# Seven-product projections: how the summed weight quarters are made, and by which engine

## The chip, the cores and the metric

One core of one Trainium2 chip runs the kernel. The metric is the device time of one execution in microseconds (us). TensorE multiplies, VectorE, ScalarE and GpSimd work elementwise, SyncE issues plain loads, and the 16 DMA engines move data; accumulating transfers (destination += source) are issued by GpSimd.

## The reference

Two decoder-like blocks on 512 tokens of width 1024, all in fp32: a first block (gated linear attention, dilated attention, MLP, an embedding gate) and a second block (mLSTM with stick-breaking attention, then a pooling layer). The part that matters is in `even_layer`: the projections that make the gates o and z of the mLSTM, two products of the normalised activations h (512 x 1024) with columns of one weight:

```
u = h @ w_in_ab                      # (512, 1024) @ (1024, ...)
o, z = 1024 columns each of u        # gates of the mLSTM's output
a = head_rmsnorm(sigmoid(o) * mlstm(q, k, v, ...)) * silu(z)
```

## The kernel before

Every fp32 matmul is made of three passes in a reduced format: each operand is split into a high part and a low part (the rest), and TensorE adds hi x hi, hi x lo, lo x hi. Weights come as blocks of 128 x 512 (256 KB). A block is loaded (SyncE, L605) into one of `RING` = 8 slots of `w_raw`, cast to `w_hi` by ScalarE (L766), and GpSimd subtracts that from the raw block to make `w_lo`, in two halves of 256 columns (`rest`, L713). `w_hi` and `w_lo` have 8 slots too; a cast of block b waits until TensorE has used block b - 8 (`wait_used`), a load until the low part of the block 8 places earlier in the ring is made (`wait_lo`). Each engine runs its queue in the order in which it is written; `prepare` and `prepared_to` say how far ScalarE's casts have to be at a place of its queue.

The gates o and z are made in another way. For each of the two, a class `Seven` splits the 1024 x 1024 weight into quarters q11, q12, q21, q22 (each 4 blocks) and the activations likewise, and replaces eight quarter products by seven, in the order B11, T1, T2, B21, T3, B22, T4. Their right operands are q11, q11+q12, q11+q12+q22, q21, q12+q22, q22, q11+q12+q22+q21. A product is 4 blocks x 2 token tiles x 3 passes = 24 matmuls (L2472 to L2474). Two products before it in TensorE's order have used its eight slots.

How the right operands are made before:

- `kept` (4 blocks in the arena) is loaded with q11 (L615) and is B11. When B11's low part of block k is made, GpSimd issues an accumulating DMA of q12 into it (`weight_sums`, L744), which gives T1; when T1's low part is made, another of q22, which gives T2. Each is waited for by the cast (`kept_summed`).
- B22 (q22) and T3's q12 come through the ring; VectorE adds the second to the first (`add_t3`, L2048).
- B21 is loaded into `b21`; VectorE adds it to `kept` for T4 (`add_t4`, L2053).
- All 28 low parts of a slab are made by VectorE (`rests`, L2063), the sums between them.

The partial results pass between products: ScalarE copies B11's result into the banks of T2 (`b_from_a`, L1280), VectorE adds T2's result and T1's copy into the banks of B22 (`c_from_b`, L2074), and T3's result to the copy (`own_from_b`, L2081). ScalarE's gate functions (L1307) and VectorE's products (L2096, L2101) take the four quarters of the result. In z's slab ScalarE also computes the squares of the heads (L1342) and a root, with two table loads. In front of the two slabs stands sb_q (8 blocks of 12 matmuls), behind them sb_k, whose low parts GpSimd makes again, and in which TensorE transposes the gated result (L2498).

Of the kernel before, what the change touches and what calls it, by code (L numbers as in the profile page):

```python
# [233 lines left out]
def plan_raw(blocks):  # L234
# [4 lines left out]
    for s, j in blocks:  # L239
        kind = "seven" if isinstance(s, Seven) else "plain"  # L240
        made[kind] += 1
        lo_at.append((kind, made[kind]))
        p, k = j // 4, j % 4
        if kind == "seven" and p not in (T3, B22):
            place.append(("b21" if p == B21 else "kept", k))
            loads.append({B11: ("kept", k, 16 * (group + 1)), T1: ("kept_sum", k, 16 * (2 * group + 1)),
                          T2: ("kept_sum", k, 16 * (2 * group + 2)), B21: ("b21", k, 16 * (group + 1)),
                          T4: ("added", 0, 8 * group + 4 + k + 1)}[p])
        else:
# [4 lines left out]
            if kind == "seven" and p == T3:  # L254
                t3_loads[len(loads)] = slots[slot]
                loads.append(("added", 0, 8 * group + k + 1))
            else:
                loads.append(("ring", slot, slots[slot]))
# [4 lines left out]
def two_blocks(nc, W, out):  # L263
# [12 lines left out]
    with ctx:  # L276
# [124 lines left out]
        for s in sevens:  # L401
            s.kept, s.b21, s.own = view(0, 4, NCOL), view(10240, 4, NCOL), view(2048, 2, NCOL)
# [28 lines left out]
        kept_summed, b21_loaded = [sem(f"kept_summed{k}") for k in range(4)], [sem(f"b21_loaded{k}") for k in range(4)]  # L431
# [112 lines left out]
        def raw_of(b):  # L544

            where, at = place[b]
            return w_raw[:, at, :] if where == "ring" else (blocks[b][0].b21 if where == "b21" else blocks[b][0].kept)[:, at, :]

        def wait_raw(eng, b):
# [3 lines left out]
                        {"ring": raw_loaded, "kept": kept_loaded, "kept_sum": kept_summed, "b21": b21_loaded}[what][at], n)  # L553
# [46 lines left out]
        def _(sp):  # L600
            def load(b, src):
                if ring_no[b] >= RING:
                    wait_lo(sp, ring_order[ring_no[b] - RING])
# [4 lines left out]
            def load_seven(s):  # L608
                at = sevens.index(s)
                if s is sevens[0]:  # L610
# [78 lines left out]
        def _(pool):  # L689
# [63 lines left out]
        def _(act):  # L753
# [557 lines left out]

            o_, z_ = sevens
# [23 lines left out]
            width = D // 4  # L1336

            def head_squares(r0):
                for r in range(r0, r0 + 8):
                    sq_ = squares[:, r // 2, (r % 2) * width:(r % 2 + 1) * width]  # L1340
                    h_ = lstm_h[:, r // LSTM_HEADS, (r % LSTM_HEADS) * LSTM_HD:(r % LSTM_HEADS + 1) * LSTM_HD]
                    ins = act.activation(sq_, h_, ACT.Square, accum_out=stat[:, r:r + 1])  # L1342
                return ins

            head_squares(0)
            prepared_to(z_, T3, 3)
            step(head_squares(8))
            act.activation(root[:], stat[:], ACT.Sqrt, bias=eps_col[:, 0:1], scale=1.0 / width).then_inc(head_root_ready, 1)
# [156 lines left out]
        def _(vec):  # L1505
# [538 lines left out]
            def add_t3(s, k):  # L2044
                own, other = s.first_of(T3) + k, s.first_of(B22) + k
                vec.wait_ge(raw_loaded[place[own][1]], t3_loads[own])
                wait_raw(vec, other)
                vec.tensor_tensor(raw_of(own), raw_of(own), raw_of(other), ALU.add).then_inc(block_added, 1)  # L2048

            def add_t4(s, k):  # L2050
                wait_raw(vec, s.first_of(B21) + k)
                wait_lo(vec, s.first_of(T2) + k)
                vec.tensor_tensor(s.kept[:, k, :], s.kept[:, k, :], s.b21[:, k, :], ALU.add).then_inc(block_added, 1)  # L2053

            def rests(s, p, k):
                while seven_made[0] < s.first_of(p) + k:
                    b = seven_made[0]
                    if lo_at[b][0] == "seven":
                        own, j = blocks[b]
                        if j // 4 == B21:  # L2060
# [930 lines left out]
```

## Time and profile before

| | |
|---|---|
| median of 3 runs | 1937.35 us (1936.15 to 1937.51) |
| profiled execution, its time | 1936.78 us |
| its span | 1935.0 us |
| busy: TensorE, weight loads | 99%, 83% |
| busy: VectorE, ScalarE, GpSimd | 41%, 42%, 49% |
| mean DMA rate over the span | 96 GB/s |

The profile is of one execution. Times in it count from the start of the span; busy shares are of the whole span, and the two slabs that the change touches run from about 1239 to 1324 us of it.

### The profile page before, as it was taken

The numbers are of one execution on the slowest core, as the hardware profiler recorded it, in microseconds if no ns is written. First come the engines' busy times: TensorE is split into PE (matmuls) and PEld (weight loads), VectorE is DVE, ScalarE is ACT, GpSimd is POOL, SyncE is SP. The second block draws the span as 40 slices with busy tenths as digits, with TensorE's granted clock in tenths as the row PEclk, the third lists the DMA queues.
The fourth block names the chain that finished last, engine by engine and source line by source line (L and its number), as shares of the span: only waits on it lengthen the run. The fifth ranks groups of instructions, "written<-read, shape, count | busy, mean of one in ns | idle before, by whom it ended". The sixth has DMA issues, their size and how long they took to land.

```text
span 1935.0 us, 25859 instructions
## 1 busy us (share of the span) xinstructions
PE 1915.9 (99%) x9142; PEld 1607.0 (83%) x9142; DVE 790.0 (41%) x1264; ACT 811.0 (42%) x1585; POOL 951.1 (49%) x1237
## 2 busy tenths in 40 slices
PE   9999999999999999999999999999999999999998
PEld 7878888998888988888889888877888888888887
DVE  2430321340123223323247854766356646014652
ACT  5522443423324333333356543355456646333332
POOL 5733544534365555665545733115344455555572
PEclk9999999999999999999999999999999999999999
DMA  6342433323133323333342320554222242333331
GB/s 233 104 107 54 123 88 87 88 66 85 57 109 109 121 88 92 100 106 103 98 131 70 106 76 23 131 136 125 61 77 71 71 136 74 101 92 93 96 111 54
DMA packets 102849, 186.44 MB, mean 96 GB/s; under 512 B 11068, under 2 KB 16808, under 8 KB 102750
## 3 DMA queue, kind: packets, MB, share of 16 engines
q1 hardware_dynamic: 94676, 170.41, 30.1%
q10 hardware_dynamic: 5770, 10.49, 1.7%
q0 software_dynamic: 2304, 4.20, 1.3%
q8 instruction: 64, 1.05, 0.2%
q14 instruction: 35, 0.29, 0.0%
HBM read 179.03 MB, written 6.02 MB: 96 GB/s over the span
## 4 chain that ended last, share of the span: by engine, by line
PE 90%; DVE 5%; ACT 2%; DMA 2%; issue 1%; POOL 0%; SPq 0%; DVEq 0%; ACTq 0%; POOLq 0%
PE proj L2325 26%; PE proj L2327 26%; PE proj L2326 26%; DMA arena<-in_w_in_ab 2%; PE work L2325 1%; PE work L2326 1%; PE work L2327 1%; PE work L2896 1%; PE work L2877 1%; DVE w_lo L2063 1%; PE work L2701 1%; ACT w_hi L766 1%; PE work L2498 1%; PE work L2852 1%; PE work L2420 1%
## 5 line engine op out<-in xcount | busy, mean ns | idle before, releaser
L713 POOL TENSOR_TENSOR w_lo<-w_raw,w_hi 128x256 fp32r<-128x256 f32 x1200 | 931.9, 809 | 877.6 <-ACT w_hi L766 761.8
L2325 PE MATMUL proj<-act_hi,w_hi 128*128 128x512 f32 (+1 forms) x1312 | 495.8, 378 | 0.6 <-DVE arena L1775 0.3
L2327 PE MATMUL proj<-act_hi,w_lo 128*128 128x512 f32 (+1 forms) x1312 | 490.4, 374 | 0.0
L2326 PE MATMUL proj<-act_lo,w_hi 128*128 128x512 f32 (+1 forms) x1312 | 490.3, 374 | 0.0
L766 ACT CAST w_hi<-w_raw 128x512 fp32r<-128x512 f32 x520 | 304.1, 619 | 398.9 <-PE proj L2327 369.7
L2325 PEld LDWEIGHTS proj<-act_hi,w_hi 128*128 128x128 f32 x1312 | 247.1, 188 | 44.6 <-DVE arena L1775 0.7
L2327 PEld LDWEIGHTS proj<-act_hi,w_lo 128*128 128x128 f32 x1312 | 247.0, 188 | 44.3
L2326 PEld LDWEIGHTS proj<-act_lo,w_hi 128*128 128x128 f32 x1312 | 247.2, 188 | 43.7 <-issue 0.5
L2325 PE MATMUL proj<-w_hi,act_hi 128*128 128x512 f32 x640 | 257.5, 402 | 1.2 <-DVE arena L2187 1.0
L2327 PE MATMUL proj<-w_hi,act_lo 128*128 128x512 f32 x640 | 250.2, 391 | 0.0
L2326 PE MATMUL proj<-w_lo,act_hi 128*128 128x512 f32 x640 | 249.9, 391 | 0.0
L2325 PEld LDWEIGHTS proj<-w_hi,act_hi 128*128 128x128 f32 x640 | 128.0, 200 | 25.3 <-issue 2.1
L2325 PE MATMUL proj<-w_hi,aux_hi 128*128 128x512 f32 x368 | 146.1, 397 | 2.9 <-ACT arena L904 1.9
L2327 PEld LDWEIGHTS proj<-w_hi,act_lo 128*128 128x128 f32 x640 | 128.0, 200 | 23.1
L2326 PEld LDWEIGHTS proj<-w_lo,act_hi 128*128 128x128 f32 x640 | 128.2, 200 | 22.8 <-issue 1.0
L2327 PE MATMUL proj<-w_hi,aux_lo 128*128 128x512 f32 x368 | 143.4, 390 | 0.0
L2326 PE MATMUL proj<-w_lo,aux_hi 128*128 128x512 f32 x368 | 143.3, 389 | 0.0
L1118 ACT CAST w_hi<-w_raw 128x512 fp32r<-128x512 f32 x96 | 57.4, 622 | 126.2 <-PE proj L2327 125.9
L1823 DVE TENSOR_TENSOR arena<-arena 128x512 f32<-128x512 f32 x32 | 26.3, 821 | 144.3 <-ACT arena L1088 144.3
L2307 DVE TENSOR_TENSOR arena<-arena 128x512 f32<-128x512 f32 x40 | 35.6, 890 | 120.2 <-ACT arena L1466 119.3
L2325 PEld LDWEIGHTS proj<-w_hi,aux_hi 128*128 128x128 f32 x368 | 69.1, 188 | 18.5 <-POOL w_lo L713 3.5
L2326 PEld LDWEIGHTS proj<-w_lo,aux_hi 128*128 128x128 f32 x368 | 69.1, 188 | 14.8 <-issue 0.7
(396 smaller groups left out, 2241.9 us busy)
## 6 DMA issues: line engine op xcount, KB each, us to landing
w_raw<-in_w_in SPq DMA_DIRECT2D x154, 256.0 KB, 2.7
w_raw<-in_w_in_ab SPq DMA_DIRECT2D x130, 256.0 KB, 2.7
w_raw<-in_w_mlp SPq DMA_DIRECT2D x128, 256.0 KB, 2.8
w_raw<-in_w_in_c SPq DMA_DIRECT2D x64, 256.0 KB, 2.7
w_raw<-in_w_out_ab SPq DMA_DIRECT2D x32, 256.0 KB, 2.8
w_raw<-in_w_out_c SPq DMA_DIRECT2D x32, 256.0 KB, 2.8
w_raw<-in_w_o_gla SPq DMA_DIRECT2D x16, 256.0 KB, 2.7
w_raw<-in_w_out SPq DMA_DIRECT2D x16, 256.0 KB, 2.7
```

The source lines that it names most:

```text
L713: ins = pool.tensor_tensor(w_lo[:, slot, c], raw_of(b)[:, c], w_hi[:, slot, c].bitcast(F32), ALU.subtract)
L766: act.copy(w_hi[:, b % RING, :], raw_of(b)).then_inc(hi_ready, 1)
L1118: act.copy(w_hi[:, b % RING, :], raw_of(b)).then_inc(hi_ready, 1)
L1823: vec.tensor_tensor(relu_sq[:, c % 2, :], relu[:, c, :], relu[:, c, :], ALU.mult).then_inc(squared, 1)
L2063: vec.tensor_tensor(w_lo[:, b % RING, :], raw_of(b), w_hi[:, b % RING, :].bitcast(F32), ALU.subtract)\
L2307: step(vec.tensor_tensor(dst[:, POOL_PAD:], src[:, POOL_PAD:], src[:, POOL_PAD - back:PADDED - back], ALU.add))
L2325: pe.matmul(out_, a_hi, b_hi, start=first, stop=False)
L2326: pe.matmul(out_, a_hi, b_lo, start=False, stop=False)
L2327: return pe.matmul(out_, a_lo, b_hi, start=False, stop=last)
L2420: ins = pe.transpose(work[:, 2 * (m % 2) + b, (k % 4) * P:(k % 4 + 1) * P], normed_x[name][:, m, k * P:(k + 1) * P], ident[:])
L2498: ins = pe.transpose(work[:, k % 4, m * P:(m + 1) * P], src[:, m, c:c + P], ident[:])
L2701: ins = pe.matmul(work[:, 3, t], att_v[g][:, kb, h * HD:(h + 1) * HD], att_pt[g][:, at * P:(at + 1) * P], start=(g == 0 and n == 0), stop= ...
```

## The change

The right operands are the same; how they are made, and by whom, differs.

- B11 and B21 are loaded through the ring, as is T3's first part. `kept` is loaded with q11 for T1 alone, so q11 is loaded twice. z has a `kept` of its own (place 14336 of the arena).
- GpSimd accumulates q12 into `kept` for T1 as soon as the load is in, and q22 onto T3's ring slot as soon as that load is in.
- T2 = `kept` + q22 (`held`, loaded for B22) on VectorE (`add_t2`), when T1's low part is made. T4 = `kept` + the ring block of B21 (`add_t4`), now in front of T3's low parts.
- The low parts of B21 and B22 are made by GpSimd; those of B11, T1, T2, T3, T4 by VectorE.
- SyncE loads in the order B11, `kept`, `held`, B21, T3 for o, and B11, `kept`, B21, `held`, T3 for z. A load into B21's slot waits for `add_t4` too.
- ScalarE's squares are spread over four places, four each, in regions that are free there.

```diff
-        super().__init__(name, q11 + q12 + q22 + q21 + q12 + q22 + q21, 4)
+        super().__init__(name, q11 + q11 + 4 * [None] + q21 + q12 + q22 + 4 * [None], 4)
+        self.added = {T1: q12, T3: q22}
...
+        maker = "plain" if kind == "plain" or p in (B21, B22) else "seven"
+        made[maker] += 1
+        lo_at.append((maker, made[maker]))
...
-            s.kept, s.b21, s.own = view(0, 4, NCOL), view(10240, 4, NCOL), view(2048, 2, NCOL)
+        for s, kept_at in zip(sevens, (0, 14336)):
+            s.kept, s.held, s.own = view(kept_at, 4, NCOL), view(10240, 4, NCOL), view(2048, 2, NCOL)
...
+                    before_ = ring_order[ring_no[b] - RING]
+                    s, j = blocks[before_]
+                    if isinstance(s, Seven) and j // 4 == B21:
+                        sp.wait_ge(block_added, 8 * sevens.index(s) + 4 + j % 4 + 1)
+                    wait_lo(sp, before_)
...
+                ring_loads(B11)
+                if at == 0:
                     sp.wait_ge(proj_full, end("lstm_core"))
                 for k in range(4):
-                    if s is not sevens[0]:
-                        wait_lo(sp, sevens[at - 1].first_of(T4) + k)
-                    sp.dma_start(s.kept[:, k, :], s.sources[k]).then_inc(kept_loaded[k], 16)
-                for p in (T3, B22):
-                    for k in range(4):
-                        load(s.first_of(p) + k, s.sources[4 * p + k])
+                    sp.dma_start(s.kept[:, k, :], s.sources[4 * T1 + k]).then_inc(kept_loaded[k], 16)
+                if at:
+                    ring_loads(B21)
                 for k in range(4):
-                    if s is not sevens[0]:
-                        sp.wait_ge(block_added, 8 * at - 4 + k + 1)
-                    sp.dma_start(s.b21[:, k, :], s.sources[4 * B21 + k]).then_inc(b21_loaded[k], 16)
+                    if at:
+                        wait_lo(sp, sevens[at - 1].first_of(B22) + k)
+                    sp.dma_start(s.held[:, k, :], s.sources[4 * B22 + k]).then_inc(held_loaded[k], 16)
+                if at == 0:
+                    ring_loads(B21)
+                ring_loads(T3)
...
             def weight_sums(s):
-                for p in (T1, T2):
+                for k in range(4):
+                    pool.wait_ge(kept_loaded[k], 16 * (sevens.index(s) + 1))
+                    pool.dma_start(s.kept[:, k, :], s.added[T1][k], accum_op=ALU.add).then_inc(kept_summed[k], 16)
+                for k in range(4):
+                    b = s.first_of(T3) + k
+                    pool.wait_ge(raw_loaded[place[b][1]], t3_loads[b])
+                    pool.dma_start(raw_of(b), s.added[T3][k], accum_op=ALU.add).then_inc(ring_summed[k], 16)
+                for p in (B21, B22):
                     for k in range(4):
-                        wait_lo(pool, s.first_of(p - 1) + k)
-                        pool.dma_start(s.kept[:, k, :], s.sources[4 * p + k], accum_op=ALU.add).then_inc(kept_summed[k], 16)
+                        b = s.first_of(p) + k
+                        pool.wait_ge(hi_ready, b + 1)
+                        rest(b).then_inc(lo_ready, 1)
...
             gate(o_, 2, ACT.Sigmoid, lstm_gated)
+            head_squares(0)
             prepared_to(z_, T1, 3)
             gate(o_, 3, ACT.Sigmoid, lstm_gated)
+            head_squares(1)
             prepared_to(z_, T2, 3)
             b_from_a(z_)
+            head_squares(2)
             prepared_to(z_, B21, 3)
             own_from_c(z_)
-            act.wait_ge(lstm_gated, 2 * MT)
+            prepared_to(z_, T3, 3)
+            ins = head_squares(3)
             act.preload_act_table_set("sqrt_and_others")
...
+            def add_t2(s, k):
+                wait_raw(vec, s.first_of(B22) + k)
+                wait_lo(vec, s.first_of(T1) + k)
+                vec.tensor_tensor(s.kept[:, k, :], s.kept[:, k, :], s.held[:, k, :], ALU.add).then_inc(block_added, 1)
...
+                    own, j = blocks[b]
+                    if isinstance(own, Seven) and j // 4 == B21:
+                        vec.wait_ge(raw_loaded[place[b][1]], loads[b][2])
+                        add_t4(own, j % 4)
...
-                        if j // 4 == T3:
-                            add_t4(own, j % 4)
+                        if j // 4 == T1:
+                            add_t2(own, j % 4)
```

## Rows read from the trace of the kernel before

**Rows 1.** The page, part 4: the chain's shares by engine.

```profile
PE 90%; DVE 5%; ACT 2%; DMA 2%; issue 1%; POOL 0%; SPq 0%; DVEq 0%; ACTq 0%; POOLq 0%
```

**Rows 2.** TensorE's waits, 1214 to 1345: line, releaser, total us, times, longest.

```profile
PE proj L2472 <- ACT proj L1280: 4.5, 1, 4.5
PE proj L2472 <- DVE proj L2074: 1.3, 2, 1.1
```

**Rows 3.** TensorE's timeline: start us, us, line, operation [idle before <-releaser].

```profile
1239.00 0.39 PE L2472 MATMUL work<-w_hi,act_hi 128*128 128x512 f32 x1
...
1244.44 0.39 PE L2472 MATMUL proj<-w_hi,aux_hi 128*128 128x512 f32 x1
...
1261.23 0.47 PE L2472 MATMUL proj<-w_hi,aux_hi 128*128 128x512 f32 x1 [0.22 <-DVE proj L2074]
...
1288.34 0.39 PE L2474 MATMUL proj<-w_hi,aux_lo 128*128 128x512 f32 x1
...
1293.20 0.77 PE L2472 MATMUL proj<-w_hi,aux_hi 128*128 128x512 f32 x1 [4.47 <-ACT proj L1280]
...
1297.87 0.39 PE L2474 MATMUL proj<-w_hi,aux_lo 128*128 128x512 f32 x1
...
1307.52 0.47 PE L2472 MATMUL proj<-w_hi,aux_hi 128*128 128x512 f32 x1 [1.10 <-DVE proj L2074]
...
1323.96 0.39 PE L2325 MATMUL proj<-act_hi,w_hi 128*128 128x512 f32 x1
```

**Rows 4.** Windows: busy us (x count) of PE, PEld, DVE, ACT, POOL; PEclk, DMA.

```profile
1288.00:1298.00 10.00, 5.53 (x16) 4.09 (x15) 6.48 (x11) 6.34 (x12) 0.16 (x1) 0.66 0.62 148
1239.00:1324.00 85.00, 79.21 (x338) 64.29 (x337) 60.38 (x98) 54.54 (x116) 14.63 (x18) 0.96 0.52 122
```

**Rows 5.** The chain that ended last, 1236 to 1330: start us, us, what.

```profile
1274.76 8.85 DMA arena<-in_w_in_ab
...
1287.30 6.82 DMA arena<-in_w_in_ab
...
1297.31 1.28 ACT L1335
...
1303.99 3.22 ACT arena L1342 x16
```

**Rows 6.** Transfers, issue to landing: plain into arena; L744 accumulates; L622 (b21).

```profile
arena<-in_w_in_ab SPq DMA_DIRECT2D x16, 256.0 KB, 5.3
...
DMA to landing us min/median/max: 4.2/6.6/9.1
...
DMA to landing us min/median/max: 5.8/9.3/15.7
```

**Rows 7.** VectorE's timeline at L2074 of z.

```profile
1306.68 1.29 DVE L2074 TENSOR_TENSOR proj<-proj,arena 128x512 f32<-128x512 f32 x2
```

**Rows 8.** In a row: VectorE's rests, ScalarE's casts, GpSimd's issues of accumulates.

```profile
1232.98 2.49 DVE L2063 TENSOR_TENSOR w_lo<-arena,w_hi 128x512 fp32r<-128x512 f32 x4
...
1250.70 2.19 ACT L766 CAST w_hi<-arena 128x512 fp32r<-128x512 f32 x4 [0.48 <-DMA arena<-in_w_in_ab]
...
1233.98 3.71 POOL L744 DMA_DIRECT2D arena<-in_w_in_ab  x4 [39.15 <-DVE w_lo L2063]
```

**Rows 9.** SyncE's queue: loads of B11 of o.

```profile
1217.42 1.75 SPq L615 DMA_DIRECT2D arena<-in_w_in_ab  x4
```

**Rows 10.** GpSimd's and VectorE's timelines, and L2101's durations (min/median/max ns).

```profile
1181.44 1.44 POOL L713 TENSOR_TENSOR w_lo<-w_raw,w_hi 128x256 fp32r<-128x256 f32 x2 [4.40 <-ACT w_hi L766]
...
L2101 DVE SCALAR_TENSOR_TENSOR arena<-arena,rstd x16: 475/956/976, 1312.6 to 1329.5; 128x256 f32<-128x256 f32 x16
...
1319.75 14.79 POOL L713 TENSOR_TENSOR w_lo<-w_raw,w_hi 128x256 fp32r<-128x256 f32 x18 [31.59 <-ACT w_hi L766]
...
1559.29 9.06 POOL L713 TENSOR_TENSOR w_lo<-w_raw,w_hi 128x256 fp32r<-128x256 f32 x13
...
1565.20 5.50 DVE L2182 TENSOR_TENSOR arena<-arena 128x512 f32<-128x512 f32 x4
```

More of the change, by code:

```diff
@@ L240, in plan_raw @@
         kind = "seven" if isinstance(s, Seven) else "plain"
-        made[kind] += 1
-        lo_at.append((kind, made[kind]))
         p, k = j // 4, j % 4
[L244 to L248, printed above, removed]
+        maker = "plain" if kind == "plain" or p in (B21, B22) else "seven"
+        made[maker] += 1
+        lo_at.append((maker, made[maker]))
+        if kind == "seven" and p in (T1, T2, B22, T4):
+            place.append(("held" if p == B22 else "kept", k))
+            loads.append({T1: ("kept_sum", k, 16 * (group + 1)), T2: ("added", 0, 8 * group + k + 1),
+                          B22: ("held", k, 16 * (group + 1)), T4: ("added", 0, 8 * group + 4 + k + 1)}[p])
         else:
@@ L430, in two_blocks @@
         kept_loaded = [sem(f"kept_loaded{k}") for k in range(4)]
-        kept_summed, b21_loaded = [sem(f"kept_summed{k}") for k in range(4)], [sem(f"b21_loaded{k}") for k in range(4)]
+        kept_summed, ring_summed = [sem(f"kept_summed{k}") for k in range(4)], [sem(f"ring_summed{k}") for k in range(4)]
+        held_loaded = [sem(f"held_loaded{k}") for k in range(4)]
         block_added = sem("block_added")
@@ L546, in raw_of @@
             where, at = place[b]
-            return w_raw[:, at, :] if where == "ring" else (blocks[b][0].b21 if where == "b21" else blocks[b][0].kept)[:, at, :]
+            return w_raw[:, at, :] if where == "ring" else (blocks[b][0].held if where == "held" else blocks[b][0].kept)[:, at, :]
         def wait_raw(eng, b):
@@ L552, in wait_raw @@
             eng.wait_ge(block_added if what == "added" else
-                        {"ring": raw_loaded, "kept": kept_loaded, "kept_sum": kept_summed, "b21": b21_loaded}[what][at], n)
+                        {"ring": raw_loaded, "kept_sum": kept_summed, "ring_sum": ring_summed, "held": held_loaded}[what][at], n)
         def wait_used(eng, block):
@@ L1310, in prepared_to, with head_squares @@
                 prepare(s.first_of(p) + k)
+            def head_squares(quarter):
+                act.wait_ge(lstm_gated, 2 * quarter + 2)
+                for m in range(2):
+                    tokens, i = (0, 2, 0, 2)[quarter] + m, (0, 1, 1, 0)[quarter]
+                    for h in (2 * i, 2 * i + 1):
+                        at, r = head_squares_at[quarter] + (2 * m + h % 2) * LSTM_HD, LSTM_HEADS * tokens + h
+                        ins = act.activation(view(at, LSTM_HD), lstm_h[:, tokens, h * LSTM_HD:(h + 1) * LSTM_HD], ACT.Square,
+                                             accum_out=stat[:, r:r + 1])
+                return ins
             o_, z_ = sevens
@@ L1327, in _ @@
             gate(o_, 2, ACT.Sigmoid, lstm_gated)
+            head_squares(0)
             prepared_to(z_, T1, 3)
             gate(o_, 3, ACT.Sigmoid, lstm_gated)
+            head_squares(1)
             prepared_to(z_, T2, 3)
             b_from_a(z_)
+            head_squares(2)
             prepared_to(z_, B21, 3)
             own_from_c(z_)
-            act.wait_ge(lstm_gated, 2 * MT)
+            prepared_to(z_, T3, 3)
+            ins = head_squares(3)
             act.preload_act_table_set("sqrt_and_others")
[L1336 to L1348, printed above, removed]
+            step(ins)
+            act.activation(root[:], stat[:], ACT.Sqrt, bias=eps_col[:, 0:1], scale=4.0 / D).then_inc(head_root_ready, 1)
             act.preload_act_table_set("silu_and_others")
@@ L2042, in _ @@
             seven_made = [sevens[0].first]
[L2044 to L2048, printed above, removed]
+            def add_t2(s, k):
+                wait_raw(vec, s.first_of(B22) + k)
+                wait_lo(vec, s.first_of(T1) + k)
+                vec.tensor_tensor(s.kept[:, k, :], s.kept[:, k, :], s.held[:, k, :], ALU.add).then_inc(block_added, 1)
             def add_t4(s, k):
-                wait_raw(vec, s.first_of(B21) + k)
                 wait_lo(vec, s.first_of(T2) + k)
-                vec.tensor_tensor(s.kept[:, k, :], s.kept[:, k, :], s.b21[:, k, :], ALU.add).then_inc(block_added, 1)
+                vec.tensor_tensor(s.kept[:, k, :], s.kept[:, k, :], raw_of(s.first_of(B21) + k), ALU.add).then_inc(block_added, 1)
             def rests(s, p, k):
@@ L2057, in rests @@
                     b = seven_made[0]
+                    own, j = blocks[b]
+                    if isinstance(own, Seven) and j // 4 == B21:
+                        vec.wait_ge(raw_loaded[place[b][1]], loads[b][2])
+                        add_t4(own, j % 4)
                     if lo_at[b][0] == "seven":
-                        own, j = blocks[b]
-                        if j // 4 == B21:
-                            add_t3(own, j % 4)
                         vec.wait_ge(hi_ready, b + 1)
```

9 lines of the change are left out of this document (5 added, 4 removed).

## The prediction

> **What bounds the kernel now.** I read the page first: TensorE holds 90% of the chain that ended last [rows 1]. So the kernel is bound by matmuls, and only an edit that takes a gap out of TensorE's stream, or puts one in, moves the time. Next I asked for TensorE's waits around the two seven-product slabs. Three show a releaser and matter: 4.5 us for ScalarE's copy at L1280, and twice VectorE's sum at L2074, 1.3 us in all [rows 2].
>
> The timeline of TensorE gives the price [rows 3]. One product is 24 matmuls; B11 of o runs from 1239.00 to 1244.44, 5.44 us, with no gap. Fourteen products at this pace are 14 x 5.44 = 76.2 us. They took from 1239.00 to 1323.96 (first matmul of sb_k), 84.96 us. So 8.8 us are lost here. T2 of z should have followed at 1288.57 and came at 1293.20 (4.63 us). Its 12th matmul started at 1297.87: 11 took 4.67 us in place of 2.49, since the granted clock was 0.66 in this stretch [rows 4], between the levels of 1.2 and 2.4 GHz, after 4.6 us without a matmul (2.18 us). T3 of z came at 1307.52; T2 had 13 matmuls of 0.227 to go at 1297.87 and ended at 1300.8, B21 one product later, 1306.26 (1.26 us), T3 of o at 1261.23 in place of 1260.85 (0.38 us). The rest, 8.80 - 8.45 = 0.35 us, is mostly the first matmul behind a wait, which takes 0.1 us longer.
>
> What was late? The chain says it for T2 of z [rows 5]: an accumulating transfer of T2, issued at 1274.76, lands 8.85 us later, then come a cast, a rest, and the next accumulate, whose transfer takes 6.82 us from 1287.30; only behind its cast stands the copy L1280 in ScalarE's queue. Before, T2's accumulate into `kept` may start only when T1's low part is made, which itself waits for T1's accumulate: two transfers of 4.2 to 9.1 us, median 6.6 [rows 6], in series with the rests, and they have 5.44 us a product. T3 of z and of o are late for another reason: L2074 stands in VectorE's queue behind interleaved sums and rests; it ran at 1306.68 [rows 7], though the product it waits for, T2, had ended at 1300.8. In z those rests also waited for casts that stood behind ScalarE's squares, 3.22 us a run of eight [rows 5].
>
> **The change part by part.** Let product p start at S(p) = 1239.00 + 5.44 p (o: B11 is 0 to T4 6; z: B11 is 7 to T4 13). The w_hi slot of block k of p frees when block k of p - 2 has been used, at S(p-2) + 1.36 (k+1). From then to its use there are 10.88 - 1.36 = 9.5 us. In a row a cast costs 2.19 / 4 = 0.55 us, a rest on VectorE 2.49 / 4 = 0.62, its sums the same, an accumulate's issue on GpSimd 3.71 / 4 = 0.93 [rows 8]. This lead is what each edit has to fit in.
>
> 1. *T1 alone is accumulated, from its own copy.* GpSimd waits for `kept_loaded` in place of T1's predecessor's rest. For o the loads go out from 1217.4 as now [rows 9] and land in 5.3 us at the median [rows 6]; the accumulates (0.9 us each to issue, 4.2 to 9.1 to land) are in by 1235; the slots free from S(0) - 3 x 2.72 = 1230.8, and TensorE wants T1 at 1244.4. For z, `kept` has its own place and no wait. GpSimd is free for it behind the rests of B22 of o, some 1265; four issues of 0.9 and 9.1 us end at 1273 to 1278; the slots free from S(6) + 1.36 = 1273.0; TensorE wants block 0 at 1282.5 and block 3 at 1286.6. Nothing late.
>
> 2. *T2 = T1 + q22 on VectorE.* Four sums of 0.6 us replace a transfer of 6.6 and its waits. T2 of z: last T1 rest some 1281.5, sum to 1282.2, slots of B11 of z free from 1278.5 to 1282.5, casts done by some 1283.5, seed copies of L1280 right behind B11's end at 1282.5 by 1285, wanted at S(9) = 1288.0. The 4.6 us gap goes, and with it the 2.18 us of slow clock.
>
> 3. *T3's accumulate is made ahead, into the ring.* Loads wait for rests of B11, 1269 to 1273 in z, land by 1278, accumulate in by some 1291 at the worst; slots free from S(9) + 1.36 = 1289.4, wanted at 1298.8. GpSimd waits for these loads in its queue, and behind them stand the rests of B21, whose casts come from 1284: not late by it.
>
> 4. *Rests of B21 and B22 go to GpSimd.* VectorE loses 16 of its 56 rests and keeps its number of sums, 16: 16 x 0.62 = 9.9 us less in a stretch where it is busy for 60.4 of 85.0 us [rows 4]. GpSimd takes 32 halves, 1.44 us a pair alone [rows 10], 23 us in all, in four bursts of some 6 us, beside 16 issues as now. It was busy for 14.6 of 85.0. A pair takes 1.44 us and TensorE uses a block each 1.36, but four blocks of burst against 9.5 us of lead fall behind by 0.3 only. The sums L2074 now find no T3 or T4 sum in front, and no squares before the casts they stand behind (the third of T3, some 1292.8 in z); they run when T2's product ends, S(3) and S(10), are done 1.3 us later, and are wanted 5.44 us after that end. The 1.26 and 0.38 us go.
>
> 5. *Two-input work of both engines at once.* In the trace of before the seven-product stretch has none; the nearest rows are outside. L2101 (128x256) took 0.475 us alone and 0.956 at the median, 12 of them beside GpSimd's rests [rows 10]; 18 of those rests took 14.79 us, 0.82 each in place of 0.72. So one VectorE instruction beside one of GpSimd costs some 0.5 us more. And from 1565.20 four 128x512 sums took 5.50 us, where four in a row take 2.5 [rows 8], while GpSimd ran 13 halves without a pause until 1568.35: the first was held for up to 3 us. The Trainium skill (SBUF — State Buffer, Who interferes with whom) says that a VectorE instruction with two SBUF inputs and a GpSimd instruction that reads SBUF exclude each other, whichever starts first, and it advises against running them together. By that rule each VectorE instruction in a burst would wait for one GpSimd half, 0.7 us, at most: some 24 instructions, 17 us of VectorE, none of it on the path. The trace agrees with it in the 0.956 row and is worse in the four sums. Bounds: below nothing (VectorE has little to do in a burst, its four T4 sums, wanted 10 us later), above, a whole burst, 6 us, in front of the last T3 rest of z. That rest is cast only at some 1298 (ScalarE has the squares and two table loads of 1.28 us in front [rows 5]), is wanted at 1302.9, and held for the burst comes at 1303.5 to 1304: 0.5 to 1.5 us late. I take zero on the path, since its cast ends before that of B22's first block.
>
> 6. *Squares in four parts on ScalarE.* The same 16 instructions, 0.40 us each, 1.6 a part. The last part, the root and the table loads (1.28 us each) stand between T3's third cast, 1292.8, and its fourth, which is then at 1298; wanted 1302.9. Before, the squares took two runs of 3.2 us between casts. Nothing on the path. If the cover is gone, each us over 4 of further delay is one on the end.
>
> 7. *Eight more plain loads*, 256 KB each. The queue moved the stretch at 122 GB/s on average [rows 4] and 2.1 MB more in 76 us is 28 GB/s. SyncE issues them ahead of need: B21 and B11 for z at 1248 to 1261, wanted from 1267. B11 of o is now in front of the wait for lstm_core in SyncE's queue and behind it nothing new waits. Zero.
>
> Behind the stretch the gates of z come earlier relative to T4's end than before, and the stages after are TensorE's as before: nothing. Sum against the profiled execution: span 1935.0, time 1936.78, so 1.78 us lie around it; gain 4.63 + 2.18 + 1.26 + 0.38 + 0.35 = 8.8; 1936.78 - 8.8 = 1928.0. The median of the runs is 0.57 above the profiled one, so 1928.55.
>
> **The rivals.** *A: GpSimd's bursts hold VectorE* (edit 5) past a rest's lead. For it: the four sums at 1565.20. Against: at the bursts VectorE's next wanted rest is 3 to 5 us off. One or two waits of 1 to 3 us: 1930 to 1934. *B: an accumulate still ends too late*, in z, where GpSimd issues it only behind B22's rests. It decides when T1 of z lands more than 15 us behind its issue at 1265: 9.1 is the longest of the accumulates, but plain loads in the crowd of before took up to 15.7 [rows 6]. With that and GpSimd 3 us late by edit 5 the gap is 3.5 us and the slow clock 2: 1928.5 + 5.5 = 1934; with a little in o too, up to 1936. *C: the gain is given back later*: the stretch is 8.8 us shorter, and sb_k waits for its weights. Against: its slots free with the rests of B21 and T3 of z, over 15 us ahead. 1937. *D, slower:* VectorE has a backlog as it meets each of the four bursts, so each holds TensorE for a burst of 5.7 us: 1928.55 + 4 x 5.7 = 1951. It decides when a burst costs more than 8.8 / 4 = 2.2 us beyond the lead. Against: VectorE would be busy for some 51 of 76 us.
>
> **How the numbers follow.** Forecast 0.74, its own range 1927 to 1930; A 0.11; B 0.06; C 0.04; D 0.05. Time 1928.5. The range from 1927.0 to 1934.0 holds the forecast and A and leaves out 0.15. What can be told from no change here is 0.2%, 3.9 us. Faster (under 1933.5): forecast and A, 0.85. Same: B and C, 0.10. Slower: D, 0.05.
>
> **What would show it.** sb_k's first matmul at 1315.2, if the slabs start at 1239.0; no wait of TensorE for L1280's or L2074's line; granted clock 1.0 throughout; T2's casts following the slots, not a transfer; 40 VectorE rests in place of 56, 1232 GpSimd halves in place of 1200. A wait of TensorE for a rest, with VectorE instructions over 1.2 us in it, is A; a cast waiting for an accumulating transfer at a product's start is B. Wrong would be a GpSimd pair beside VectorE at over 2.7 us through a whole burst, or accumulates over 12 us.

## The result, and the profile after

The changed kernel took 1925.35 us at the median of four runs beside 1936.75 us for four of the kernel before: ratio 0.9942, 95% interval 0.9926 to 0.9958, so 0.4 to 0.7% faster. A second set on another call gave 1925.46 beside 1935.97 us, ratio 0.9946 (0.9933 to 0.9960). The forecast was faster, at 1928.5 us with a range from 1927.0; the measured time lies 1.7 us under the range and 3.1 us under the forecast. The direction came out as forecast, and so did the end of the gaps in TensorE's stream; the size did not.

The page of the changed kernel, parts 1 and 4 (the chain answers to [rows 1]):

```profile
span 1923.6 us, 25891 instructions
...
PE 1912.3 (99%) x9142; PEld 1605.7 (83%) x9142; DVE 789.7 (41%) x1248; ACT 812.9 (42%) x1585; POOL 984.4 (51%) x1269
...
PE 97%; DVE 1%; ACT 1%; DMA 0%; issue 0%; SPq 0%; POOL 0%; DVEq 0%; ACTq 0%
```

TensorE now holds 97% of the chain, the transfers and VectorE nearly nothing. TensorE's timeline has no idle time in front of any matmul of the slabs. The trace has 40 low parts on VectorE and 1232 halves on GpSimd, where the trace of before has 56 and 1200, as forecast. These rows answer to [rows 3]; the columns are start, duration, line, operation:

```profile
17.04 0.47 PE L2348 MATMUL proj<-w_hi,aux_hi 128*128 128x512 f32 x1 [0.82 <-ACT arena L925]
...
1237.89 0.39 PE L2495 MATMUL work<-w_hi,act_hi 128*128 128x512 f32 x1
...
1286.86 0.39 PE L2495 MATMUL proj<-w_hi,aux_hi 128*128 128x512 f32 x1
...
1297.73 0.39 PE L2495 MATMUL proj<-w_hi,aux_hi 128*128 128x512 f32 x1
...
1314.06 0.39 PE L2348 MATMUL proj<-act_hi,w_hi 128*128 128x512 f32 x1
...
1316.78 1.47 PE L2521 MATMUL work<-ident,arena 128*128 128x128 f32 x12
```

The slabs run from 1237.89 to 1314.06: 76.17 us, where they took 84.96 and the forecast had 76.2. T2 of z starts at 1286.86, T3 of z at 1297.73, each on the grid of 5.44 us. The window over them answers to [rows 4]:

```profile
1238.00:1314.00 76.00, 76.00 (x337) 62.94 (x336) 58.64 (x78) 55.30 (x114) 44.48 (x49) 1.00 0.58 144
```

The granted clock is 1.00. VectorE is busy for 58.6 us of 76 (60.4 of 85 before; the prediction had some 51 of 76), GpSimd for 44.5 (14.6 before).

Laid matmul beside matmul (both traces have 9142), the changed kernel gains on the kernel before in four places only: 1.12 us at 17 us, 8.79 us in the slabs, 0.41 us at the first transposes behind sb_k (L2498, now L2521), 1.16 us at 1573 us of the old trace. The sum is 11.5 us, and the spans differ by 1935.0 - 1923.6 = 11.4. The forecast had the second of these to 0.01 us and gave the other three nothing.

### The profile page after: what moved, and what is told of

It is laid out like the page before. It is cut to its first block, busy times and chain, and to the rows that moved or that the text cites. A ratio compares the mean times of both kernels' runs of the same rounds, so it can differ in the third digit from the quotient of the medians.

```text
span 1923.6 us, 25891 instructions
## 1 busy us (share of the span) xinstructions
PE 1912.3 (99%) x9142; PEld 1605.7 (83%) x9142; DVE 789.7 (41%) x1248; ACT 812.9 (42%) x1585; POOL 984.4 (51%) x1269
## 3 DMA queue, kind: packets, MB, share of 16 engines
q8 instruction: 64, 1.05, 0.2%
## 4 chain that ended last, share of the span: by engine, by line
PE 97%; DVE 1%; ACT 1%; DMA 0%; issue 0%; SPq 0%; POOL 0%; DVEq 0%; ACTq 0%
PE proj L2348 27%; PE proj L2350 27%; PE proj L2349 27%; PE work L2348 1%; PE work L2349 1%; PE work L2350 1%; PE proj L2497 1%; PE proj L2496 1%; PE proj L2495 1%; PE work L2919 1%; PE work L2900 1%; PE work L2521 1%; PE work L2724 1%; PE work L2875 1%; PE proj L2867 1%; PE work L2443 1%
## 5 line engine op out<-in xcount | busy, mean ns | idle before, releaser
L726 POOL TENSOR_TENSOR w_lo<-w_raw,w_hi 128x256 fp32r<-128x256 f32 x1216 | 951.2, 816 | 859.0 <-ACT w_hi L787 743.3
L787 ACT CAST w_hi<-w_raw 128x512 fp32r<-128x512 f32 x528 | 309.6, 619 | 430.1 <-PE proj L2350 395.7
L1139 ACT CAST w_hi<-w_raw 128x512 fp32r<-128x512 f32 x96 | 57.4, 622 | 126.2 <-PE proj L2350 125.9
```

Source lines behind the costliest of these rows:

```text
L726: ins = pool.tensor_tensor(w_lo[:, slot, c], raw_of(b)[:, c], w_hi[:, slot, c].bitcast(F32), ALU.subtract)
L787: act.copy(w_hi[:, b % RING, :], raw_of(b)).then_inc(hi_ready, 1)
L1139: act.copy(w_hi[:, b % RING, :], raw_of(b)).then_inc(hi_ready, 1)
```

## The experiments

Twelve runs: each of the two kernels once more, and ten edits of one of them. A table first, since most verdicts need the same four numbers of each profile: the length of the slabs (first matmul of B11 of o to the first of sb_k), from there to the first transposes, how long the four gating sums of VectorE behind the second attention took (L2182 before, L2205 changed), and the start of the matmul that waits for the load of x. Then the span and the median of all executions, and the median of the kernel before that was timed beside it, all in us.

| kernel | slabs | to transposes | four sums | x's matmul | span | median | before beside it |
|---|---|---|---|---|---|---|---|
| before (first profile) | 84.96 | 3.13 | 5.50 | 18.16 | 1935.0 | | |
| repeat_before | 84.99 | 3.13 | 4.40 | 17.09 | 1932.8 | 1936.23 | 1935.97 |
| changed (first profile) | 76.17 | 2.72 | 4.41 | 17.04 | 1923.6 | 1925.35 | 1936.75 |
| repeat_after | 76.15 | 2.72 | 4.41 | 16.82 | 1923.4 | 1925.46 | 1935.97 |
| vec_rests | 76.16 | 2.72 | 4.41 | 17.01 | 1923.6 | 1926.33 | 1935.97 |
| squares_block | 76.84 | 4.08 | 5.50 | 18.03 | 1927.8 | 1929.23 | 1935.97 |
| t2_accum | 76.26 | 2.72 | 4.41 | 16.84 | 1923.5 | 1926.49 | 1936.08 |
| t2_sum_only | 79.42 | 3.15 | 5.48 | 17.55 | 1928.6 | 1930.19 | 1936.08 |
| order_only | 84.96 | 3.65 | 4.42 | 17.51 | 1933.8 | 1936.30 | 1936.08 |
| pool_four | 82.51 | 2.73 | 5.48 | 18.10 | 1932.1 | 1933.32 | 1936.08 |
| after_hold | 76.16 | 2.72 | 2.73 | 17.45 | 1923.8 | 1925.36 | 1935.69 |
| before_hold | 84.95 | 3.15 | 2.78 | 18.66 | 1934.3 | 1934.95 | 1935.69 |
| small_two | 78.95 | 4.08 | 4.35 | 17.25 | 1927.9 | 1929.64 | 1935.69 |
| squares_only | 83.79 | 2.72 | 4.34 | 17.31 | 1931.5 | 1933.65 | 1935.69 |

**repeat_before and repeat_after**: both kernels as they are.

> The kernel before, unchanged, profiled once more and timed. In the two profiles that there are, TensorE's matmuls of the changed kernel run ahead of those of the kernel before by 1.1 us from 17 us on (a load of x), by 8.9 us more behind the seven-product slabs, by 0.4 us at the first transposes of z, and by 1.1 us more at 1573 us (VectorE's four sums beside a burst of GpSimd). Theory 1: the steps at 17 and at 1573 us are chance of one execution; then this profile, laid beside that of the kernel before, differs by 0 to 1.2 us at one or both of these places, and the span lies anywhere from 1932.7 to 1935. Theory 2: the change makes them; then this profile agrees with that of the kernel before within 0.2 us at both.

> The changed kernel, unchanged, for a paired time with a narrow interval. Theory 1 (the two steps outside the slabs are chance of one execution): the paired difference is what the slabs and the transposes give, 8.9 + 0.4 = 9.3 us, ratio 0.9952. Theory 2 (the change makes them all): 11.4 us, ratio 0.9941.

Of repeat_before, TensorE's matmul behind x and VectorE's sums (timelines of both engines):

```profile
17.09 0.47 PE L2325 MATMUL proj<-w_hi,aux_hi 128*128 128x512 f32 x1 [0.80 <-ACT arena L904]
...
1564.03 4.40 DVE L2182 TENSOR_TENSOR arena<-arena 128x512 f32<-128x512 f32 x4
```

It is quicker at both steps, with the very code that was slow there in the first profile: there the chain of waits showed x's load as the first row below, here as the second.

```profile
3.30 7.08 DMA x<-in_x
```

```profile
3.30 6.02 DMA x<-in_x
```

Its span is 2.2 us shorter (1932.8 for 1935.0), its own time 1934.54 for 1936.78, and its slabs are as long as before, 84.99. So the steps at 17 and at 1573 us come without the change, in some executions of the same code: theory 1. (That the change alters how often they come is not excluded by it.) The change's own part is 8.84 us in the slabs and 0.41 us behind them, and repeat_before laid beside repeat_after gives 1932.8 - 1923.4 = 9.4 us, of which 0.27 us are at x. The paired medians differ by 10.5 us, ratio 0.9946 (0.9933 to 0.9960), whose interval holds both 9.3 us (0.9952) and 11.4 us; which of the two theories is right is decided by the profiles, not by the times.

**vec_rests**: the low parts of B21 and B22 back on VectorE.

> The changed kernel with the low parts of B21 and B22 on VectorE again; all else as changed. Theory 1 (the prediction's: the long gap is the second accumulate in series, the short ones are L2074's place in VectorE's queue behind sums and rests): the place of L2074 in the queue is still behind T3's first three rests only, VectorE has 51 + 10 us of work in 76 us, so nothing or up to 1 us is lost: 1925.4 to 1926.4. Rival (handing the 16 rests to GpSimd is what frees VectorE): the two short gaps come back, 1.6 us, or more if the sums L2075 push T3's rests: 1927 or more.

```diff
-        maker = "plain" if kind == "plain" or p in (B21, B22) else "seven"
+        maker = kind
...
-                for p in (B21, B22):
-                    for k in range(4):
-                        b = s.first_of(p) + k
-                        pool.wait_ge(hi_ready, b + 1)
-                        rest(b).then_inc(lo_ready, 1)
```

76.16 us of slabs, no wait of TensorE, ratio to before 0.9948 (0.9932 to 0.9963), beside 0.9946 with the move. Handing the 16 rests to GpSimd gives nothing that shows. The 0.9 us between the medians is not in the profile (spans 1923.6 and 1923.4).

**squares_block**: ScalarE's squares in two runs of eight again.

> The changed kernel with ScalarE's squares in two runs of eight again, as before the change, the first behind a wait for all eight gated tiles. Theory 1 (the squares delayed T3's casts of z and through them L2074): T3's second and third cast of z come 3.2 us and a table load later, at some 1296, L2074 at 1297, wanted at 1297.7: a gap of 0 to 0.7 us. Rival (the squares stand on the path as soon as they are in runs): 1.3 us or more as in the kernel before.

```diff
-            head_squares(0)
...
-            head_squares(1)
...
-            head_squares(2)
             prepared_to(z_, B21, 3)
             own_from_c(z_)
+            act.wait_ge(lstm_gated, 2 * MT)
+            act.preload_act_table_set("sqrt_and_others")
+            head_squares(0)
+            head_squares(1)
             prepared_to(z_, T3, 3)
+            head_squares(2)
             ins = head_squares(3)
-            act.preload_act_table_set("sqrt_and_others")
```

TensorE's waits in and behind the slabs (line, releaser: us, times, longest):

```profile
PE work L2522 <- DVE arena L2125: 0.8, 1, 0.8
PE proj L2496 <- DVE arena L2105: 0.2, 1, 0.2
```

The slabs are 0.68 us longer, inside theory 1's range but not by its mechanism: L2098 ran at 1296.81 and had ended by 1298.1, before T3 of z was due at 1298.73, and the wait is one in T4 for T3's own sum, own_from_b (L2105). The first transposes come 1.36 us later, because L2125's gates end later. So on the changed kernel the spread squares carry 2.0 us. The medians differ by 3.8 us. The profile has 1.2 us more at x and the slow form of the sums, 1.1 us:

```profile
1557.88 5.50 DVE L2206 TENSOR_TENSOR arena<-arena 128x512 f32<-128x512 f32 x4
```

Whether these two are chance here too is open: all four executions, 1928.5 to 1929.5 us, are at least 3.3 us above the quickest of repeat_after.

**t2_accum**: T1 ahead as changed, T2 by a second accumulating transfer as before.

> The changed kernel with T2 made by a second accumulating DMA again, issued by GpSimd when T1's low part is made; T1's accumulate stays ahead of use, the rest is as changed. Theory 1 (the long gap of 4.6 us and its 2.2 us of slow clock are two accumulates and two rests in series within two products; with the first one ahead, one accumulate of 4 to 9 us behind T1's rests of 1274 to 1281 lands at 1283 to 1288, and L1280's copies stand behind its third block): 0 to 3 us of the 6.8 come back, 1925.5 to 1928.5. Rival (the sum on VectorE is what removes the gap): all 6.8 us come back, 1932.3.

```diff
+                for k in range(4):
+                    wait_lo(pool, s.first_of(T1) + k)
+                    pool.dma_start(s.kept[:, k, :], s.added[T3][k], accum_op=ALU.add).then_inc(kept_summed[k], 16)
...
-                        if j // 4 == T1:
-                            add_t2(own, j % 4)
```

GpSimd's and ScalarE's timelines in z's slab:

```profile
1275.02 2.65 POOL L759 DMA_DIRECT2D arena<-in_w_in_ab  x3 [8.07 <-DVE w_lo L2089]
...
1281.71 0.62 ACT L790 CAST w_hi<-arena 128x512 fp32r<-128x512 f32 x1 [2.01 <-DMA arena<-in_w_in_ab]
1282.97 0.62 ACT L790 CAST w_hi<-arena 128x512 fp32r<-128x512 f32 x1 [0.64 <-DMA arena<-in_w_in_ab]
1283.50 1.06 ACT L1304 COPY proj<-work 128x512 f32<-128x512 f32 x2
```

The three first accumulates of T2 go out from 1275.02, the third block is cast at 1282.97, and the copies L1304 follow at 1283.50, 3.2 us ahead of T2. 76.26 us of slabs, ratio 0.9954 (0.9938 to 0.9971), 1926.5 us: theory 1. The sum on VectorE is not needed once T1 is ahead and the other edits are in.

**t2_sum_only**: on the kernel before, T2 by a sum on VectorE, T1's accumulate still behind B11's rest.

> The kernel before with one edit of the change: T2 = T1 + q22 by a sum on VectorE, from B22's ring block, in place of the second accumulating DMA; T1's accumulate still waits for B11's rest. Theory 1: the 4.6 + 2.2 us go, the short gaps at L2074 stay or grow, since VectorE has eight sums more: 1929 to 1930.5. Rival (T1's accumulate, behind B11's rest, is late by itself): at least 3 us of gap stay: 1932 or more.

```diff
+            def add_t2(s, k):
+                wait_raw(vec, s.first_of(B22) + k)
+                wait_lo(vec, s.first_of(T1) + k)
+                vec.tensor_tensor(s.kept[:, k, :], s.kept[:, k, :], raw_of(s.first_of(B22) + k), ALU.add).then_inc(block_added, 1)
```

TensorE's waits:

```profile
PE proj L2479 <- DVE proj L2081: 1.6, 1, 1.6
PE proj L2479 <- DVE w_lo L2068: 0.6, 1, 0.6
```

79.42 us: 5.5 us less than before. The wait for L1280 is gone, with its slow clock; the one for L2074 (here L2081) stays, 1.6 us, and a new one of 0.6 us comes in front of T1's last block of z, whose rest stands behind the new sums. Ratio 0.9969 (0.9958 to 0.9981), 1930.2 us: in theory 1's range. So T2's sum alone takes the long gap away on the kernel before, and T1 ahead does it without that sum on the changed one; the change has both. T1 ahead alone, on the kernel before, was not run.

**order_only**: on the kernel before, L2074 ahead of T3's rests.

> The kernel before with the order of VectorE's queue changed alone: L2074 stands in front of T3's rests in both slabs (a sum of T3 goes ahead of it, the sums of T4 and the rests behind). Theory 1 (L2074's place made the two short gaps): 1.3 + 0.4 = 1.6 us less than before, 1934.4. Rival (T3's rests are then late in place of it): no change, 1936.0.

```diff
-            rests(o_, T3, 3)
+            rests(o_, B21, 4)
             c_from_b(o_)
...
             rests(z_, B21, 3)
+            rests(z_, B21, 4)
+            c_from_b(z_)
             rests(z_, T3, 3)
-            c_from_b(z_)
             head_scales(2)
```

```profile
PE proj L2473 <- ACT proj L1280: 5.5, 2, 4.4
PE work L2499 <- DVE arena L2101: 0.8, 1, 0.8
```

No wait for L2074 is left, in o 0.36 us and in z 1.78 us less than repeat_before. But the slabs are 84.96 us long: T2 of o now waited 1.05 us for the copy behind an accumulating transfer, where it came less than 0.1 us late in the two profiles of before. T2 of z still waited its 4.4 us, and behind the wait its 24 matmuls took 8.3 us at a granted clock of 0.65, where repeat_before has 7.1 us at 0.76 (5.44 at full clock): 1.2 us more. Ratio 1.0005 (0.9996 to 1.0015): no change, the figure of the rival, but not its reason. One profile each can't tell how much of this is chance; the medians, of 10 and 22 executions, show no gain.

**pool_four**: GpSimd makes the low parts of T3 and T4 too.

> The changed kernel with GpSimd making the low parts of T3 and T4 as well, so four products of seven in place of two: 64 halves in 76 us, 1.44 to 2.0 us a block against a block each 1.36 us of TensorE. Theory 1 (one block falls behind by 0.1 to 0.7 us, and a lead of 9.5 us covers a burst of one product but not four in a row): the four bursts follow each other from B21's first cast to T4's end, 16 blocks behind by 16 x 0.4 = 6 us, of which the lead covers most: 0 to 4 us more, 1925.5 to 1929.5; T1 of z gets its accumulate 5 us later. Rival (as soon as VectorE and GpSimd meet, both double): 16 x 1.3 = 20 us behind, over 10 us more: 1935 or more.

```diff
-        maker = "plain" if kind == "plain" or p in (B21, B22) else "seven"
+        maker = "plain" if kind == "plain" or p in (B21, T3, B22, T4) else "seven"
...
-                for p in (B21, B22):
+                for p in (B21, T3, B22, T4):
```

GpSimd's timeline, and what TensorE's weight loads waited for:

```profile
1246.64 12.70 POOL L726 TENSOR_TENSOR w_lo<-w_raw,w_hi 128x256 fp32r<-128x256 f32 x16 [6.20 <-ACT w_hi L787]
1259.30 9.79 POOL L726 TENSOR_TENSOR w_lo<-arena,w_hi 128x256 fp32r<-128x256 f32 x14
...
1274.63 3.54 POOL L756 DMA_DIRECT2D arena<-in_w_in_ab  x4
...
1293.45 13.39 POOL L726 TENSOR_TENSOR w_lo<-w_raw,w_hi 128x256 fp32r<-128x256 f32 x16 [7.48 <-ACT w_hi L787]
```

```profile
PEld proj L2495 <- POOL w_lo L726: 4.1, 11, 0.6
PEld proj L2495 <- DVE w_lo L2086: 3.2, 4, 2.0
```

The slabs take 82.51 us, 6.3 more, between the two theories: a burst of 16 halves takes 12.7 us, 0.79 each, not twice 0.72, so the rival's doubling is not there, but theory 1 was too low as well. It left out the other thing in GpSimd's queue. T1's accumulates of z go out at 1274.63 where they did at 1263.45, 11.2 us later and not 5, and T1's casts wait for their landing. ScalarE's timeline:

```profile
1280.45 0.62 ACT L787 CAST w_hi<-arena 128x512 fp32r<-128x512 f32 x1 [2.89 <-DMA arena<-in_w_in_ab]
1282.37 0.62 ACT L787 CAST w_hi<-arena 128x512 fp32r<-128x512 f32 x1 [1.30 <-DMA arena<-in_w_in_ab]
1284.29 0.62 ACT L787 CAST w_hi<-arena 128x512 fp32r<-128x512 f32 x1 [1.30 <-DMA arena<-in_w_in_ab]
```

TensorE's first waits in z, at 1285.7 and 1289.0, are for VectorE's low parts of these blocks (L2086), the second also because the fourth cast stands behind gates and squares in ScalarE's queue, until 1287.57. Rival B of the prediction is this: an accumulate late behind GpSimd's rests. T1 of z carries 2.6 of the 6.3 us; the other 3.7 come from B21 on, where TensorE waits for GpSimd's own low parts. Two products of rests keep both away, four do not. Ratio 0.9986 (0.9976 to 0.9995): some three quarters of the change's gain are gone (2.8 us left of 10.5).

**squares_only**: on the kernel before, the squares in four parts.

> The kernel before with ScalarE's squares in four parts, as changed, and nothing else. Theory 1 (with the long gap in place, T2 of z ends at 1300.8 and L2074 waits in VectorE's queue for T3's third rest, whose cast stood behind eight squares until 1302): the 1.3 us of gap in front of T3 of z goes and the long gap stays: 1934.7. Rival (VectorE's sums alone hold L2074): 1936.0.

TensorE's waits:

```profile
PE proj L2475 <- ACT proj L1280: 3.5, 1, 3.5
PE proj L2475 <- DVE w_lo L2066: 0.6, 1, 0.6
```

83.79 us of slabs and 2.72 us to the transposes: 1.20 and 0.41 us less than repeat_before. No wait for L2074 (here L2077) in z is left, as theory 1 had it; T2's long wait is 3.5 us here, with 0.6 us for a rest in front of it. The slow clock behind it costs 1.0 us more than in repeat_before (T2's 24 matmuls take 8.1 us at 0.66), which is why 1.20 us is left of the 1.8 of the gap. Ratio 0.9989 (0.9979 to 0.9998), 1933.65 us, where theory 1 had 1934.7. It takes the gap of z away as order_only does; o's, 0.3 us, stays.

**small_two**: on the kernel before, t2_sum_only's and order_only's edits together.

> The kernel before with two small edits together: T2 by a sum on VectorE in place of the second accumulate, and L2074 in front of T3's rests; no GpSimd rests, no ring for B11 and B21, squares as before. Theory 1 (the long gap is the accumulates in series, the short ones are the order of the queue, and both go by these two): 6.8 + 1.6 = 8.4 us less than before, less the 0.3 to 0.8 us of T2's own rests behind the sums: 1927.8 to 1928.5. Rival (the squares hold T3's casts and keep the short gap of z): 1929.3 to 1930.

78.95 us of slabs, 6.0 less than before, but 4.08 us to the transposes, 0.95 more. Ratio 0.9966 (0.9953 to 0.9979), 1929.6 us: the rival's figure. The wait at L2074 is gone, and what it and the long gap hid stands in the open: rests of T1 of z behind sums (1.15 us in two waits), T3's last rest, whose cast came only at 1302.93, behind the squares, the root and its table load (0.3 us), and the gates of z, also behind the squares (0.95 us). So the rival is right that the squares cost something here, though not at L2074.

**after_hold and before_hold**: GpSimd waits at block 4 of the first even_out1 slab until the four gating sums are done.

> The changed kernel, with GpSimd held at one place behind the slabs: before it makes the low part of block 4 of the first even_out1 slab it waits until VectorE's four gating sums (L2205, two inputs from SBUF) are done. In four of six profiles these sums took 4.41 us, one for one with GpSimd's halves, in two they took 5.50 or more, the first held 3.69 us until GpSimd's burst had ended, and TensorE came 1.1 us later. Theory 1 (the two engines take turns or not, by chance, and it costs 1.1 us when not): the sums take 2.5 to 3.2 us every time, no execution has the step of 1.1 us, TensorE waits for none of it: median 0 to 1 us lower than the changed kernel's, 1924.5 to 1925.5. Rival (GpSimd's hold makes its low parts late): 1 to 3 us higher.

> The kernel before with the same hold of GpSimd at its gating sums L2182 and nothing else. Theory 1 (this place costs the kernel before 1.1 us in some executions): sums in 2.5 to 3.2 us, median 0.3 to 1.1 us lower than before, 1935.0 to 1935.7. Rival (the hold costs as much as it gives): 1936.1 or more.

```diff
+            hold_at = by_name["even_out1"][0].first + 4
-            plain_rests(sevens[-1].first + sevens[-1].n, n_blocks)
+            plain_rests(sevens[-1].first + sevens[-1].n, hold_at)
+            pool.wait_ge(yb_ready, 2 * MT)
+            plain_rests(hold_at, n_blocks)
```

The four sums in after_hold:

```profile
1555.19 2.73 DVE L2208 TENSOR_TENSOR arena<-arena 128x512 f32<-128x512 f32 x4
```

2.73 us, in place of 4.41 or 5.50, and TensorE waits for nothing there. Against the changed kernel the median does not move (1925.36 and 1925.46 us; its first set had 1925.35). Both profiles of that kernel have the form of 4.41 us, and TensorE waits for nothing there either. On the kernel before it is 1934.95 us beside 1935.69, ratio 0.9993 (0.9983 to 1.0002): the expected direction and size, but the interval still holds no change. No kernel here beats the changed one.

## Why the prediction was wrong in size and right in mechanism

- **The step that failed: the sum's base.** The prediction took its gain off one execution, 1936.78 us ("Sum against the profiled execution"), with "the stages after are TensorE's as before: nothing", and added 0.57 us for the median. That execution held two steps of 1.1 us that the same code is without in repeat_before (1934.54 us, the same slabs). The three terms account for the miss of 3.2 us: 1936.78 - 1934.54 = 2.24 us of base, the 0.57 us, and 0.41 us at the transposes. In other words, 1934.54 - 8.84 - 0.41 = 1925.3 us, which is what the changed kernel takes in its profiles (1925.31 and 1925.18). The range's lower end, 1927.0, took in the bounds of the change's costs and none of the base's own scatter, 1934.5 to 1939.5 us in repeat_before's eleven executions. Only part of the 2.8 us of base and median is a bad draw: 1.4 us, by the median of 1936.0 us that a set of 15 executions gives in place of the 1937.35 of three. That median is itself 1.4 us above the quiet profile, where the changed kernel's is 0.3 us above its own; this surplus went too, and why is open (last point).
- **Edits 1 to 3, the long gap.** Right: 4.63 and 2.18 us are gone, T2 of z came on the grid. The prediction named one accumulate in series with another as the cause, and t2_accum and t2_sum_only bear that out: with either of the two out of the series the 4.6 us are gone. So one of the two edits would have done for the long gap (t2_sum_only, without T1 ahead, keeps 0.6 us in T1 of z). The first accumulates of z went out at 1263.45 (forecast some 1265), and the eight of T1 landed in 4.3 to 10.0 us, where the bound had been 9.1. GpSimd's timeline, and L756's landing times (min/median/max):

```profile
1219.29 1.02 POOL L756 DMA_DIRECT2D arena<-in_w_in_ab  x1 [25.57 <-DMA arena<-in_w_in_ab]
...
1245.66 8.04 POOL L726 TENSOR_TENSOR w_lo<-w_raw,w_hi 128x256 fp32r<-128x256 f32 x8 [6.18 <-ACT w_hi L787]
1256.53 6.97 POOL L726 TENSOR_TENSOR w_lo<-arena,w_hi 128x256 fp32r<-128x256 f32 x8 [2.83 <-ACT w_hi L787]
1263.45 3.56 POOL L756 DMA_DIRECT2D arena<-in_w_in_ab  x4
...
1284.92 8.77 POOL L726 TENSOR_TENSOR w_lo<-w_raw,w_hi 128x256 fp32r<-128x256 f32 x8 [6.53 <-ACT w_hi L787]
1297.57 6.86 POOL L726 TENSOR_TENSOR w_lo<-arena,w_hi 128x256 fp32r<-128x256 f32 x8 [3.88 <-ACT w_hi L787]
```

```profile
DMA to landing us min/median/max: 4.3/8.2/10.0
```

- **Edit 4, GpSimd's rests.** None of it is on the path, as forecast, and none of it is a gain either (vec_rests); the four bursts took 6.9 to 8.8 us and not 6. L2074's successor L2097 ran at 1293.02, 0.7 us behind T2's end at 1292.3, and was wanted at 1297.7. For the gap of z the prediction named two delays of L2074, the sums in VectorE's queue and the squares in front of the casts, and counted on both edits. Either is enough: squares_only takes the gap away with the queue as it was, order_only and squares_block are without it with the squares in runs. For o's gap, 0.4 us, the sums in the queue are one cause of two: it stays in squares_only (0.3 us) and is gone in order_only, but also in t2_sum_only, where L2074 (there L2081) has the same sums and rests in front and runs 19.6 us behind the start of the slabs in place of 21.4, since T2's low parts no longer wait for the second accumulate.
- **Edit 5, both engines on SBUF.** Taken as zero on the path, and it was. It is there off the path: the four T4 sums took 4.70 us where four low parts of the same size took 2.5 alone [rows 8], three T3 rests 3.52. T3's last rest, the place of rival A, ran at 1297.08, wanted at 1301.8. VectorE's and ScalarE's timelines:

```profile
1284.96 4.70 DVE L2075 TENSOR_TENSOR arena<-arena,w_raw 128x512 f32<-128x512 f32 x4
1289.58 3.52 DVE L2086 TENSOR_TENSOR w_lo<-w_raw,w_hi 128x512 fp32r<-128x512 f32 x3
1293.02 1.28 DVE L2097 TENSOR_TENSOR proj<-proj,arena 128x512 f32<-128x512 f32 x2
...
1297.08 0.69 DVE L2086 TENSOR_TENSOR w_lo<-w_raw,w_hi 128x512 fp32r<-128x512 f32 x1 [1.75 <-ACT w_hi L787]
```

```profile
1280.93 1.25 ACT L1301 COPY proj<-work 128x512 f32<-128x512 f32 x2
...
1296.35 0.62 ACT L787 CAST w_hi<-w_raw 128x512 fp32r<-128x512 f32 x1
```

  By the rule of the Trainium skill (SBUF — State Buffer, Who interferes with whom) an instruction would wait for one GpSimd half, 0.7 us at most. The trace agrees with it here: a sum takes 1.2 us, 0.5 more than the 0.68 it takes alone. The hold of 3.7 us told of below goes beyond it, and the measurement decides. The prediction also has the page advise against running the two together; its words are milder, to schedule whichever is off the critical path (Summary: rules for kernel authors).
- **Edit 6, the squares.** Its cast of T3's last block came at 1296.35, forecast 1298, with the slabs starting 1.1 us earlier than assumed. Its value was underrated: "nothing on the path" is right for the cost, but squares_block prices the gain at 0.68 us in the slabs and 1.36 us at the transposes.
- **Behind the stretch: a term of 0 that was 0.41 us.** The prediction wrote that the gates of z come earlier relative to T4's end, and then took nothing for it. The spread squares do it: squares_only, made from the kernel before, has 2.72 us to the transposes in place of 3.13, and squares_block, made from the changed one, 4.08 in place of 2.72.
- **Rivals.** A and C did not happen, C not even in part. B did not happen in the change, but pool_four makes it happen. D did not happen either: pool_four, with twice the GpSimd rests, lost 6.3 us in the slabs and is still not slower than before.
- **Open.** The medians of a pair differ by 10.5 us, the quiet profiles by 9.4. The times show that the kernel before scatters more, 1934.4 to 1937.8 us in one set of 22 beside 1925.2 to 1927.6 in five of the changed one. Its copies stand behind transfers whose landing varies (order_only's 1.05 us in o is one case), and that may be the reason, but no profile here counts how often. This is argued, not shown.

## What to carry to other kernels

Before a gain is taken off one profiled execution, ask which of its waits would be there in the next: a wait behind a load at the start, or behind two engines that met, may be chance, and a second profile of the kernel before costs less than any experiment; put the base's scatter into the range. When an instruction in an in-order queue is late, name what stands in front of it on every engine in the chain: VectorE's sums and ScalarE's squares both delayed L2074, and removing either was enough. Of two edits that each remove one of two delays in series, the second can earn nothing, so test each alone before both are kept.

## What was not expected of the hardware

VectorE's four gating sums of 128x512, beside a burst of GpSimd's halves, come in one of two forms. GpSimd's timeline at these sums, in the profile of before and in repeat_before:

```profile
1557.21 11.13 POOL L713 TENSOR_TENSOR w_lo<-w_raw,w_hi 128x256 fp32r<-128x256 f32 x16 [0.65 <-ACT w_hi L766]
```

```profile
1556.09 12.95 POOL L713 TENSOR_TENSOR w_lo<-w_raw,w_hi 128x256 fp32r<-128x256 f32 x16 [0.65 <-ACT w_hi L766]
```

In the second they take turns: the sums last 0.97, 1.22, 1.22 and 1.22 us, and GpSimd's halves beside them 1.19 us in place of 0.73. In the first the first sum lasts 3.69 us, through five halves of GpSimd at their normal 0.74 us (the one that ran when the sum started and the four behind it, the end of the burst), and the next three sums last 0.68 us each. Of the twelve profiles in which GpSimd does not wait for the sums, eight have turns and four the long hold (before, squares_block, t2_sum_only, pool_four), over kernels of either kind. Code that had the hold in one profile had turns in the next (before and repeat_before). The hold makes the four sums 1.1 us longer than turns do, and in all four of its profiles TensorE then waits 1.0 us for VectorE, in the others not at all. What decides between the two is open.
